# A two-stack transformer kernel: the FFN's down product runs two groups behind gate and up, and its first groups go through HBM

## Chip, cores and metric

One core of a Trainium2 chip runs one program. The metric is device microseconds (us) from start to end of an execution, median of three; lower is better. All arithmetic is float32; matmul operands are split into a high and a low part of a shorter type, and each product is three matmuls.

## Reference

Two stacks of two layers each work on one sequence of 256 tokens of width 1024. A layer is an FFN, a mixing part (attention and a gated recurrence, not touched here) and a second FFN, so there are eight FFNs. Cut to what matters:

```python
def swiglu(h, w_gate, w_up, w_down):            # w_gate, w_up: 1024 x 2816; w_down: 2816 x 1024
    return (jax.nn.silu(h @ w_gate) * (h @ w_up)) @ w_down

def hybrid_layer(x, ...):
    x = x + 0.5 * swiglu(rmsnorm(x, ffn1_norm), ffn1_wg, ffn1_wu, ffn1_wd)
    x = x + mixing(rmsnorm(x, mix_norm))        # projections, attention, recurrence, w_out
    x = x + 0.5 * swiglu(rmsnorm(x, ffn2_norm), ffn2_wg, ffn2_wu, ffn2_wd)
    return x
```

## The kernel before

All weights come from HBM in one stream of **units** of 1 MB (128 x 2048 floats), in the order of use. A unit passes four engines. SP (`load`, L317) starts its DMA into one of five `raw` buffers, once DVE has finished with the unit that held the buffer (`lo_done`). ACT (`split`, L815) copies it to one of three `w_hi` slots, once PE has used the unit three earlier (`used`). DVE (`split`, L1215) writes the remainder into `w_lo`. PE waits for `lo_done` and runs the unit's 24 matmuls of 512 columns.

An FFN has 11 groups of 256 hidden columns (`GROUPS`). Group g has three units: `front` and `back`, the two halves of gate and up over the 1024 inputs, and `down`, its 256 rows of the down matrix. `ffn_use` numbers them in the stream. Each engine's program is written out by hand and runs in that order; semaphores tie the engines together. The first FFN's units are called unit 0, 1, 2 and so on in this text.

Between gate/up and down, a group's 256 x 256 activations have to be computed and turned. ACT (`gates`, L877) takes the sigmoid from the two PSUM banks into `gate_s`, DVE (`gated`, L1260) multiplies twice and leaves `act` (semaphore `a_ready`). Then there are two ways to turn it:

- groups in `TURNED`: PE transposes `act` with four 128 x 128 matmuls into the bank `PT` (`turn_act`, L528). Before the change these are groups 0 and 10 of every FFN and group 1 of the first, 17 in all.
- groups in `EXCHANGED`: SP sends `act` to HBM (`spill`) and, after that has landed, reads it back in another order (`exchange`, L338); DVE finishes with 32 x 32 transposes (`act_turn`, L1271) into `act_t`. `act_t` and `gate_s` are the same SBUF bytes, so `gates` of the next group waits until `act_low` has read `act_t`.

Either way ACT writes `act_hi` (`act_high`, L888) and DVE `act_lo` (`act_low`, L1277; semaphore `alo_ready`), on which `down` waits. SP's exchange stands in the same queue as its weight loads: while it waits for `a_ready` or for the spill to land, no load is issued.

PSUM has eight banks: `PB` (0, 1) for gate/up, `PD` (2 to 5) for the down sums (and for gate/up of group 0), `PX` (6, 7), of which bank 6 is `PT`. Before the change every group from 1 on used `PB`.

In the first FFN, three small pieces of unrelated work are put between the groups: `tables(0)` to `tables(2)` on DVE after groups 1, 4 and 7 (`DVE_TABLES_AT`) and `tables(0)`, `tables(1)` on ACT after groups 2 and 5 (`ACT_TABLES_AT`). DVE's `tables(0)` is the run of operations from L1730 to L1753, ACT's holds three table loads. At the same time POOL loads constants and 16 pieces of `rpb` through its own DMA queue, and then adds masks to them.

Of the kernel before, what the change touches and what calls it, by code (L numbers as in the profile page):

```python
# [27 lines left out]
GROUPS = FF // 256  # L28
LAYERS = 2
UNIT = 2048  # L30
SLOTS, RAW = 3, 5
# [26 lines left out]
EXCHANGED = [at for at in ALL_GROUPS if 0 < at[3] < GROUPS - 1 and at != (0, 0, 0, 1)]  # L58
# [28 lines left out]
def build(nc, stream, xt, params, final_gain, code_w, gate_w, forget_w, rpb,  # L87
          lower, positions, forget_bias, c_square, c_level, c_col, c_att, c_freq, c_sel, c_reset, spill, out):
    ctx = ExitStack()
    with ctx:  # L90
# [90 lines left out]
        XB, PT = bank[0:2] + bank[6:8], bank[6]  # L181
# [80 lines left out]
        def ffn_no(b, L, j, g):  # L262
            return (4 * b + 2 * L + j) * GROUPS + g

# [146 lines left out]
        def _(pe):  # L411
# [81 lines left out]
            def ffn(b, L, j):  # L493
# [3 lines left out]
                def front(banks, g):  # L497
# [3 lines left out]
                    if g >= 2:  # L501
                        pe.wait_ge(a_ready, 2 * ffn_no(b, L, j, g))
# [309 lines left out]
        def _(act):  # L812
# [58 lines left out]
            def ffn(b, L, j):  # L871
# [5 lines left out]
                def gates(g):  # L877
                    if g >= 1:
                        act.wait_ge(alo_ready, ffn_no(b, L, j, g))
                    for t in range(2):  # L880
                        if t == 0:
                            act.wait_ge(tile_ready, ffn_no(b, L, j, g) + 1)
                        else:
                            act.wait_ge(used, use_of("back", g) + 1)
                        src = (PD if g == 0 else PB)[t][:, 0:256]
                        fn(gate_s[:, t, :], src, ACT.Sigmoid, scale=rms[:, t:t + 1]).then_inc(sig_done, 1)  # L886

                def act_high(g):  # L888
# [3 lines left out]
                    else:  # L892
                        act.wait_ge(act_turned, spill_no(b, L, j, g) + 1)
                        src = act_t
                    fn(act_hi[g % 2][:, :, :].rearrange("p a b -> p (a b)"), src, ACT.Copy).then_inc(ahi_ready, 1)  # L895
# [29 lines left out]
                for g in range(1, GROUPS):  # L925
                    act_high(g - 1)
                    split(use_of("front", g) + SLOTS)
                    gates(g)
                    split(use_of("back", g) + SLOTS)
                    if g == GROUPS - 1:  # L930
                        act_high(g)
                        table(EXP_LN_SET)
# [8 lines left out]
                    split(use_of("down", g - 1) + SLOTS)  # L941
# [266 lines left out]
        def _(dve):  # L1208
# [44 lines left out]
            def ffn(b, L, j):  # L1253
# [6 lines left out]
                def gated(g):  # L1260
                    no = ffn_no(b, L, j, g)
                    banks = PD if g == 0 else PB
# [54 lines left out]
                for g in range(1, GROUPS):  # L1317
                    if (b, L, j, g - 1) in EXCHANGED:
                        act_turn(g - 1)
                    act_low(g - 1)  # L1320
                    split(use_of("front", g) + SLOTS)
                    gated(g)
                    if g == GROUPS - 1:
                        split(use_of("back", g) + SLOTS)
                        act_low(g)
                    else:
                        split(use_of("back", g) + SLOTS)
# [6 lines left out]
                    if g < GROUPS - 1:  # L1334
                        split(use_of("down", g - 1) + SLOTS)
# [553 lines left out]
def weight_stream(i):  # L1889
# [5 lines left out]
    for b in range(2):  # L1895
        g1, u1, d1, w_in, w_out, g2, u2, d2 = (i[k] for k in names[b])
        for L in range(LAYERS):
            def ffn(j, g, u, d):
# [12 lines left out]
                gate_up(0)  # L1911
                for n in range(1, GROUPS):
                    gate_up(n)
                    down(n - 1)
# [65 lines left out]
```

## Time and profile before

| | us |
|---|---|
| median of 3 runs (lowest, highest) | 2010.35 (2009.53, 2012.16) |
| the profiled execution: its time, its span | 2007.96, 2006.2 |
| PE busy | 1983.8 (99% of the span) |
| DVE busy | 1374.9 (69%) |
| ACT busy | 1067.5 (53%) |

PE's matmuls overlap in the records: one lasts 0.39 us and the next starts 0.23 us after it, so that a PE that always shows busy may still lose small pieces of time between starts. Times inside the trace count from the span's start. The groups of rows below are quoted by number further on.

### The profile page before, as it was taken

The page shows a single profiled execution, that of the slowest core. Times are in us where ns is not written, and L with a number is a line of the kernel's source. Part 1 is how long each engine was busy: PE and PEld are TensorE (multiplying, and loading weights), DVE is VectorE, ACT ScalarE, POOL GpSimd, SP SyncE. Part 2 cuts the span into 40 slices and gives each one's busy share as a digit, 9 for nine tenths or more (in the row PEclk, how much of TensorE's full clock was granted, in tenths as well). Part 3 has the DMA queues.
Part 4 walks back from the last instruction along what each step waited for, and adds up shares of the span by engine and source line. Part 5 has one row for each costly group of instructions (what it writes and reads, how often), then busy time and mean ns, then how long its engine had stood idle before and what let it go on. Part 6 is the DMA issues. An engine that isn't in the chain of part 4 may idle for free.

```text
span 2006.2 us, 26785 instructions
## 1 busy us (share of the span) xinstructions
PE 1983.8 (99%) x10888; PEld 1663.8 (83%) x10888; DVE 1374.9 (69%) x1688; ACT 1067.5 (53%) x1357; POOL 55.6 (3%) x73
## 2 busy tenths in 40 slices
PE   8999999999999999999999999999999999999998
PEld 7888887888888887888888898888888889888887
DVE  6666976666666696766666669766666666976665
ACT  5545676444544567544554466654455445665444
POOL 3200004000000000000000000000000000000000
PEclk9999999999999999999999999999999999999999
DMA  9765437666566543666566644256656664425662
GB/s 321 249 222 188 162 113 211 228 221 228 193 232 225 177 150 105 220 225 229 195 217 230 227 156 169 107 203 221 227 193 221 227 230 159 168 106 210 221 221 83
DMA packets 145995, 395.62 MB, mean 197 GB/s; under 512 B 81808, under 2 KB 100496, under 8 KB 103504
## 3 DMA queue, kind: packets, MB, share of 16 engines
q1 hardware_dynamic: 142832, 387.49, 55.4%
q0 software_dynamic: 2608, 6.07, 1.4%
q8 instruction: 86, 1.41, 0.3%
q10 hardware_dynamic: 432, 0.35, 0.1%
q14 instruction: 37, 0.30, 0.0%
HBM read 374.21 MB, written 19.66 MB: 196 GB/s over the span
## 4 chain that ended last, share of the span: by engine, by line
PE 87%; DVE 7%; ACT 3%; DVEq 1%; DMA 1%; issue 1%; ACTq 0%; SPq 0%
PE bank L421 83%; DVE w_lo L1219 2%; PE bank L466 1%; PE bank L589 1%; ACT w_hi L821 1%; PE bank L673 1%; DVE arena L1347 1%; PE bank L657 1%; PE bank L635 1%; DMA spill<-scratch 0%; DVE arena L1434 0%; PE bank L603 0%; PE bank L532 0%; DMA x<-xt 0%; DVEq L1435 0%
## 5 line engine op out<-in xcount | busy, mean ns | idle before, releaser
L1219 DVE TENSOR_TENSOR w_lo<-raw,w_hi 128x2048 fp32r<-128x2048 f32 x330 | 757.6, 2297 | 379.5 <-ACT w_hi L821 378.9
L821 ACT ACTIVATE w_hi<-raw 128x2048 fp32r<-128x2048 f32 x330 | 629.7, 1910 | 246.1 <-PE bank L421 242.9
L421 PE MATMUL bank<-w_hi,h_hi 128*128 128x512 f32 x1536 | 602.5, 392 | 1.3 <-DVE arena L1511 0.8
L421 PE MATMUL bank<-w_hi,h_lo 128*128 128x512 f32 x1536 | 598.3, 390 | 0.0
L421 PE MATMUL bank<-w_lo,h_hi 128*128 128x512 f32 x1536 | 598.1, 389 | 0.0
L421 PEld LDWEIGHTS bank<-w_hi,h_hi 128*128 128x128 f32 x1536 | 288.6, 188 | 64.5 <-issue 2.7
L421 PEld LDWEIGHTS bank<-w_hi,h_lo 128*128 128x128 f32 x1536 | 288.5, 188 | 60.5
L421 PEld LDWEIGHTS bank<-w_lo,h_hi 128*128 128x128 f32 x1536 | 288.7, 188 | 58.8
L421 PE MATMUL bank<-w_hi,act_hi 128*128 128x512 f32 x832 | 327.8, 394 | 2.9 <-DVE act_lo L1568 2.1
L421 PE MATMUL bank<-w_hi,act_lo 128*128 128x512 f32 x832 | 324.2, 390 | 0.0
L421 PE MATMUL bank<-w_lo,act_hi 128*128 128x512 f32 x832 | 324.0, 389 | 0.0
L886 ACT ACTIVATE scratch<-bank,rms 128x256 f32<-128x256 f32 x176 | 83.2, 474 | 206.1 <-PE bank L421 206.0
L421 PEld LDWEIGHTS bank<-w_hi,act_hi 128*128 128x128 f32 x832 | 156.2, 188 | 36.9 <-DVE act_lo L1568 2.9
L421 PEld LDWEIGHTS bank<-w_hi,act_lo 128*128 128x128 f32 x832 | 156.2, 188 | 32.8
L421 PEld LDWEIGHTS bank<-w_lo,act_hi 128*128 128x128 f32 x832 | 156.3, 188 | 31.3
L895 ACT ACTIVATE act_hi<-scratch 128x512 fp32r<-128x512 f32 x71 | 45.0, 633 | 245.2 <-DVEq L1275 245.2
L421 PE MATMUL bank<-h_hi,w_hi 128*128 128x256 f32 x576 | 165.2, 287 | 0.0
L421 PE MATMUL bank<-h_lo,w_hi 128*128 128x256 f32 x576 | 162.8, 283 | 0.0
L421 PE MATMUL bank<-h_hi,w_lo 128*128 128x256 f32 x576 | 162.7, 283 | 0.0
L421 PEld LDWEIGHTS bank<-h_hi,w_hi 128*128 128x128 f32 x576 | 110.1, 191 | 3.9 <-issue 3.4
L421 PEld LDWEIGHTS bank<-h_hi,w_lo 128*128 128x128 f32 x576 | 110.2, 191 | 0.0
L421 PEld LDWEIGHTS bank<-h_lo,w_hi 128*128 128x128 f32 x576 | 110.2, 191 | 0.0
(213 smaller groups left out, 1403.4 us busy)
## 6 DMA issues: line engine op xcount, KB each, us to landing
raw<-stream SPq DMA_DIRECT2D x331, 1024.0 KB, 4.9
spill<-scratch SPq DMA_DIRECT2D x71, 256.0 KB, 3.7
scratch<-spill SPq DMA_DIRECT2D x71, 256.0 KB, 2.6
arena<-rpb POOLq DMA_DIRECT2D x32, 96.0 KB, 9.5
x<-xt SPq DMA_DIRECT2D x4, 256.0 KB, 5.5
raw<-stream SPq DMA_DIRECT2D x2, 512.0 KB, 5.9
arena<-final_gain POOLq DMA_DIRECT2D x2, 512.0 KB, 4.4
out<-x SPq DMA_DIRECT2D x3, 256.0 KB, 2.5
```

Source lines behind the costliest of these rows:

```text
L421: last = mm(o, a, r, start=start and n == 0, stop=stop and n == len(pairs) - 1)
L466: last = nc.tensor.transpose(XB[k // 2][:, (k % 2) * T + t * P:(k % 2) * T + (t + 1) * P], source[:, t, k * P:(k + 1) * P], ident)
L589: last = mm(PD[o][half, at:at + 64], src[rows, 1, ch, 64 * n:64 * n + 64], src[rows, 0, ch, 64 * m:64 * m + 64], start=True, stop=True)
L635: last = mm(PX[e][:, 0:n], aq[rows, hp, q], ak[rows, hp, 0:n], start=True, stop=True)
L657: last = nc.tensor.transpose(turn_bank(b, i)[:, n * P:(n + 1) * P], scratch[:, i % 2, n * P:(n + 1) * P], ident)
L673: last = mm(head_bank(b, i)[64 * e:64 * e + 64, 0:P], av[:, kt, hp * P + 64 * e:hp * P + 64 * e + 64], pT[:, i % 2, (2 * e + kt) * P:(2 * ...
L821: fn(w_hi[u % SLOTS][:, :], raw[u % RAW][:, :], ACT.Copy).then_inc(hi_done, 1)
L886: fn(gate_s[:, t, :], src, ACT.Sigmoid, scale=rms[:, t:t + 1]).then_inc(sig_done, 1)
L895: fn(act_hi[g % 2][:, :, :].rearrange("p a b -> p (a b)"), src, ACT.Copy).then_inc(ahi_ready, 1)
L1219: tt(w_lo[u % SLOTS][:, :], raw[u % RAW][:, :], w_hi[u % SLOTS][:, :].bitcast(F32), ALU.subtract).then_inc(lo_done, 1)
L1347: return tt(dst, a, r, ALU.subtract)
```

## The change

`ffn_use` and `weight_stream` put the down unit of group g behind gate and up of group g + 2 instead of g + 1. The order in the first FFN, by units, was front 0, back 0, front 1, back 1, down 0, front 2, back 2, down 1, ...; it becomes front 0, back 0, front 1, back 1, front 2, back 2, down 0, front 3, back 3, down 1, ..., back 10, down 8, down 9, down 10. Gate and up use `PD` for group 0, `PB` for odd groups and `PX` for even ones from 2 on. `EXCHANGED` takes in every group but the last, so 8 groups are left in `TURNED`. On ACT and DVE, groups 1 and 2 have both weight splits ahead of the turning of the group before; later groups have one ahead of it.

```diff
-EXCHANGED = [at for at in ALL_GROUPS if 0 < at[3] < GROUPS - 1 and at != (0, 0, 0, 1)]
+EXCHANGED = [at for at in ALL_GROUPS if at[3] < GROUPS - 1]
...
-        XB, PT = bank[0:2] + bank[6:8], bank[6]
+        XB, PT = bank[0:2] + bank[6:8], bank[0]
...
             if kind == "down":
-                off = 3 * g + 4 if g < GROUPS - 1 else FFN_UNITS - 1
+                off = 3 * g + 6 if g < GROUPS - 2 else FFN_UNITS - GROUPS + g
             else:
-                off = (3 * g - 1 if g else 0) + (kind == "back")
+                off = (3 * g - 2 if g else 0) + (g == 1) + (kind == "back")
...
+        def gate_banks(g):
+
+            return PD if g == 0 else PB if g % 2 else PX
...
-                    if g >= 2:
-                        pe.wait_ge(a_ready, 2 * ffn_no(b, L, j, g))
+                    if g >= 3:
+                        pe.wait_ge(a_ready, 2 * ffn_no(b, L, j, g - 1))
...
-                front(PD, 0)
-                back(PD, 0)
-                for g in range(1, GROUPS):
-                    front(PB, g)
-                    if (b, L, j, g - 1) in TURNED:
-                        turn_act(g - 1)
-                    back(PB, g)
-                    down(g - 1, {(0, 3): lambda: turn_act(GROUPS - 1)} if g == GROUPS - 1 else {})
+                for g in range(GROUPS):
+                    front(gate_banks(g), g)
+                    back(gate_banks(g), g)
+                    if g >= 2:
+                        down(g - 2)
+                turn_act(GROUPS - 1)
+                down(GROUPS - 2)
...
                 for g in range(1, GROUPS):
+                    split(use_of("front", g) + SLOTS)
+                    if g < 3:
+                        split(use_of("back", g) + SLOTS)
                     if (b, L, j, g - 1) in EXCHANGED:
                         act_turn(g - 1)
                     act_low(g - 1)
-                    split(use_of("front", g) + SLOTS)
                     gated(g)
+                    if g >= 3:
+                        split(use_of("back", g) + SLOTS)
```

DVE in the first FFN before the change, from the gating of group 0 on. L1265/L1269 are `gated`, L1280 is `act_low`, L1219 a weight split; `raw0` here holds unit 5, `raw1` unit 6, `raw2` unit 7:

```order
L1219 TENSOR_TENSOR w_lo2<-raw0,w_hi2 128x2048 [waits hi_done]
L1265 SCALAR_TENSOR_TENSOR scratch<-bank,rms,scratch 128x256 [waits sig_done]
L1269 SCALAR_TENSOR_TENSOR scratch<-bank,rms,scratch 128x256 [waits at_ready]
L1265 SCALAR_TENSOR_TENSOR scratch<-bank,rms,scratch 128x256 [waits sig_done]
L1269 SCALAR_TENSOR_TENSOR scratch<-bank,rms,scratch 128x256
L1219 TENSOR_TENSOR w_lo0<-raw1,w_hi0 128x2048 [waits hi_done]
L1730 CAST arena<-cos_sin 128x256 [waits table_loaded]
...
L1753 TENSOR_SCALAR cos_sin<-arena 128x256 x2
L1219 TENSOR_TENSOR w_lo1<-raw2,w_hi1 128x2048 [waits hi_done]
```

and of the changed kernel (L1286 is `act_turn`, L1231 a weight split, L1744 to L1767 are `tables(0)`):

```order
L1231 TENSOR_TENSOR w_lo2<-raw0,w_hi2 128x2048 [waits hi_done]
L1231 TENSOR_TENSOR w_lo0<-raw1,w_hi0 128x2048 [waits hi_done]
L1286 STREAM_TRANSPOSE scratch<-scratch 128x4x2x32 [waits act_back]
L1286 STREAM_TRANSPOSE scratch<-scratch 128x4x2x32
L1292 TENSOR_TENSOR act_lo0<-scratch,act_hi0 128x512 [waits ahi_ready]
L1277 SCALAR_TENSOR_TENSOR scratch<-bank,rms,scratch 128x256 [waits sig_done]
...
L1744 CAST arena<-cos_sin 128x256 [waits table_loaded]
...
L1767 TENSOR_SCALAR cos_sin<-arena 128x256 x2
L1231 TENSOR_TENSOR w_lo1<-raw2,w_hi1 128x2048 [waits hi_done]
```

The turning of group 0 now waits for a DMA (`act_back`), and `tables(0)` and the split of unit 7 come behind it.

ACT at the same place before the change (L895 is `act_high`, L886 `gates`, L821 a weight split, `raw4` holds unit 9, `raw0` unit 10):

```order
L895 ACTIVATE act_hi1<-bank 128x512 [waits at_ready]
L821 ACTIVATE w_hi2<-raw3 128x2048 [waits used,raw_ready3]
L886 ACTIVATE scratch<-bank,rms 128x256 [waits tile_ready,alo_ready]
L886 ACTIVATE scratch<-bank,rms 128x256 [waits used]
L821 ACTIVATE w_hi0<-raw4 128x2048 [waits used,raw_ready4]
L833 ACT_TABLE_LOAD
...
L821 ACTIVATE w_hi1<-raw0 128x2048 [waits used,raw_ready0]
```

and of the changed kernel (L900 `act_high`, L889 `gates`, L824 a weight split):

```order
L900 ACTIVATE act_hi1<-scratch 128x512 [waits act_turned]
L889 ACTIVATE scratch<-bank,rms 128x256 [waits tile_ready,alo_ready]
L889 ACTIVATE scratch<-bank,rms 128x256 [waits used]
L836 ACT_TABLE_LOAD
L1179 ACTIVATE cos_sin<-cos_sin 128x512 [waits ang_ready]
L836 ACT_TABLE_LOAD
L1181 ACTIVATE lbt<-lbt 128x8
L836 ACT_TABLE_LOAD
L824 ACTIVATE w_hi0<-raw4 128x2048 [waits used,raw_ready4]
```

The split of unit 9 stood ahead of ACT's tables and now stands behind them.

## Rows read from the trace of the kernel before

**Rows 1.** Chain that ended last, one piece of the second FFN: start, us, what, matmuls.
```profile
339.18 155.09 PE bank L421 x684
```

**Rows 2.** Timeline of PE around two turned groups: start, us, engine, line, what [idle before].
```profile
338.35 0.39 PE L421 MATMUL bank<-w_hi,h_lo 128*128 128x512 f32 x1
...
339.73 0.39 PE L421 MATMUL bank<-w_hi,h_hi 128*128 128x512 f32 x1
...
1012.39 0.60 PE L532 MATMUL bank<-square,scratch 128*128 128x128 f32 x4
1013.18 0.50 PE L421 MATMUL bank<-w_hi,h_hi 128*128 128x512 f32 x1 [0.19 <-DVE w_lo L1219]
```

**Rows 3.** The line of the PE transposes, its instructions over the whole span.
```profile
L532 PE MATMUL bank<-square,scratch x68: 270/272/273, 28.0 to 1990.8; 128*128 128x128 f32 x68
```

**Rows 4.** Timeline of PE in the first FFN: unit 2's last matmul, unit 11's first.
```profile
27.81 0.39 PE L421 MATMUL bank<-w_hi,h_lo 128*128 128x512 f32 x1
...
73.32 0.47 PE L421 MATMUL bank<-w_hi,h_hi 128*128 128x512 f32 x1 [0.27 <-DVE scratch L1269]
```

**Rows 5.** Timeline of DVE in the first FFN.
```profile
27.04 0.48 DVE L1269 SCALAR_TENSOR_TENSOR scratch<-bank,rms,scratch 128x256 f32<-128x256 f32 x1
...
38.69 0.44 DVE L1730 CAST arena<-cos_sin 128x256 f32<-128x256 int32 x1
...
44.90 2.27 DVE L1219 TENSOR_TENSOR w_lo<-raw,w_hi 128x2048 fp32r<-128x2048 f32 x1
...
59.98 2.94 DVE L1219 TENSOR_TENSOR w_lo<-raw,w_hi 128x2048 fp32r<-128x2048 f32 x1 [4.41 <-ACT w_hi L821]
64.74 1.10 DVE L1274 STREAM_TRANSPOSE scratch<-scratch 128x256 f32<-128x256 f32 x2 [1.82 <-DMA scratch<-spill]
66.57 0.69 DVE L1280 TENSOR_TENSOR act_lo<-scratch,act_hi 128x512 fp32r<-128x512 f32 x1 [0.73 <-ACT act_hi L895]
...
71.19 0.47 DVE L1265 SCALAR_TENSOR_TENSOR scratch<-bank,rms,scratch 128x256 f32<-128x256 f32 x1
...
73.09 4.49 DVE L1219 TENSOR_TENSOR w_lo<-raw,w_hi 128x2048 fp32r<-128x2048 f32 x2
```

**Rows 6.** Timeline of ACT in the first FFN.
```profile
39.66 1.92 ACT L821 ACTIVATE w_hi<-raw 128x2048 fp32r<-128x2048 f32 x1 [3.22 <-PE bank L421]
...
53.27 1.28 ACT L833 ACT_TABLE_LOAD   x1
...
58.03 1.92 ACT L821 ACTIVATE w_hi<-raw 128x2048 fp32r<-128x2048 f32 x1
...
68.25 0.81 ACT L886 ACTIVATE scratch<-bank,rms 128x256 f32<-128x256 f32 x2
```

**Rows 7.** DMA issues, last figure us to landing: unit 8's load; an exchange at 393:402.
```profile
25.64 0.33 SPq L321 DMA_DIRECT2D raw<-stream  x1
raw<-stream SPq DMA_DIRECT2D x1, 1024.0 KB, 9.3
...
spill<-scratch SPq DMA_DIRECT2D x1, 256.0 KB, 3.6
scratch<-spill SPq DMA_DIRECT2D x1, 256.0 KB, 2.6
```

**Rows 8.** DMA queues at 38:40 (q0 is POOL's, q1 SP's): packets, MB, share.
```profile
q0 software_dynamic: 145, 0.36, 93.3%
q1 hardware_dynamic: 18, 0.08, 14.1%
```

**Rows 9.** PE's timeline, early and last; a window: length, busy by engine, clock, DMA.
```profile
11.36 0.63 PE L421 MATMUL bank<-w_lo,h_hi 128*128 128x512 f32 x1
11.79 0.63 PE L421 MATMUL bank<-w_hi,h_lo 128*128 128x512 f32 x1
...
1998.87 0.39 PE L421 MATMUL bank<-w_hi,act_lo 128*128 128x512 f32 x1
...
2002.50:2003.00 0.50, 0.00 (x0) 0.00 (x0) 0.00 (x0) 0.16 (x1) 0.00 (x0) 0.50 0.00 0
```

More of the change, by code:

```diff
@@ L884, in gates @@
                             act.wait_ge(used, use_of("back", g) + 1)
[L885 removed]
+                        src = gate_banks(g)[t][:, 0:256]
                         fn(gate_s[:, t, :], src, ACT.Sigmoid, scale=rms[:, t:t + 1]).then_inc(sig_done, 1)
@@ L894, in act_high @@
                         src = act_t
+                    if g >= 2:
+                        act.wait_ge(used, use_of("down", g - 2) + 1)
                     fn(act_hi[g % 2][:, :, :].rearrange("p a b -> p (a b)"), src, ACT.Copy).then_inc(ahi_ready, 1)
@@ L925, in ffn @@
                 for g in range(1, GROUPS):
+                    split(use_of("front", g) + SLOTS)
+                    if g < 3:
+                        split(use_of("back", g) + SLOTS)
                     act_high(g - 1)
-                    split(use_of("front", g) + SLOTS)
                     gates(g)
-                    split(use_of("back", g) + SLOTS)
+                    if g >= 3:
+                        split(use_of("back", g) + SLOTS)
                     if g == GROUPS - 1:
                         act_high(g)
+                        split(use_of("down", g - 2) + SLOTS)
                         table(EXP_LN_SET)
@@ L940, in ffn @@
                         fn(code_hi[:, :], w, ACT.Copy).then_inc(code_split, 1)
-                    split(use_of("down", g - 1) + SLOTS)
+                    if 2 <= g < GROUPS - 1:
+                        split(use_of("down", g - 2) + SLOTS)
+                    if g == GROUPS - 1:
+                        split(use_of("down", g - 1) + SLOTS)
             def evict_pair(b, L, i, t):
@@ L1261, in gated @@
                     no = ffn_no(b, L, j, g)
-                    banks = PD if g == 0 else PB
+                    banks = gate_banks(g)
                     for t in range(2):
@@ L1317, in ffn @@
                 for g in range(1, GROUPS):
+                    split(use_of("front", g) + SLOTS)
+                    if g < 3:
+                        split(use_of("back", g) + SLOTS)
                     if (b, L, j, g - 1) in EXCHANGED:
@@ L1320, in ffn @@
                     act_low(g - 1)
-                    split(use_of("front", g) + SLOTS)
                     gated(g)
+                    if g >= 3:
+                        split(use_of("back", g) + SLOTS)
                     if g == GROUPS - 1:
-                        split(use_of("back", g) + SLOTS)
                         act_low(g)
-                    else:
-                        split(use_of("back", g) + SLOTS)
+                        split(use_of("down", g - 2) + SLOTS)
                     if (b, L, j, g) in DVE_TABLES_AT:
@@ L1333, in ffn @@
                         tt(code_lo[:, :], w, code_hi[:, :].bitcast(F32), ALU.subtract).then_inc(code_split, 1)
-                    if g < GROUPS - 1:
-                        split(use_of("down", g - 1) + SLOTS)
+                    if 2 <= g < GROUPS - 1:
+                        split(use_of("down", g - 2) + SLOTS)
             def halves(ap, m):
@@ L1909, in down @@
                         out.append(rows.reshape(4, 2, 32, D).transpose(0, 2, 1, 3).reshape(P, UNIT))
-                gate_up(0)
-                for n in range(1, GROUPS):
+                for n in range(GROUPS):
                     gate_up(n)
-                    down(n - 1)
+                    if n >= 2:
+                        down(n - 2)
+                down(GROUPS - 2)
                 down(GROUPS - 1)
```

## The prediction, made blind

> **What bounds the kernel now.** I read the page's busy shares first: PE 99% of the span, everything else under 70%. Then the chain that ended last: nearly all of it is PE, in long unbroken pieces. Inside an FFN 684 matmuls take 155.09 us, 0.2267 us each [rows 1], so a unit of 24 takes 5.44 us, and nothing that only gives the other engines more slack can shorten that. The list of waits shows PE idle behind other engines only twice inside the FFNs, for 0.27 and 0.19 us [rows 2, 4]. So the change can win only the PE instructions that it removes, and can lose wherever one of the other engines becomes late. I therefore read the timelines of DVE, ACT and SP where slack is smallest: the first FFN, where `tables`, POOL's loads and the first exchanges meet.
>
> **Part 1: nine groups less transposed on PE.** 68 transposes are 17 groups [rows 3]; 8 are left. From the start of the last matmul ahead of one to that of the fourth behind it, 338.35 to 339.73 are 1.38 us where four steps of 0.2267 make 0.91 [rows 2]: a group costs 0.47 us. Two of the nine lie in the first FFN and are in part 2. Of the other seven, the one at 1012.39 gives nothing: PE stands behind it for the split of the next unit, and that unit starts at 1013.18 either way, since neither ACT nor DVE gets to that split sooner [rows 2]. Six are left: 6 x 0.47 = 2.8 us gained.
>
> **Part 2: the first FFN.** I step through it to unit 11, which is front 4 in both orders and started at 73.32 [rows 4]. Undisturbed, the units after 27.81 + 0.23 = 28.04 come every 5.44 us [rows 1, 4]: unit 4 at 38.9, unit 6 (now down 0) at 44.4, unit 7 (front 3) at 49.8, unit 9 (down 1) at 60.7, unit 11 at 71.6.
>
> Call X0 the time at which DVE starts turning group 0. It cannot be sooner than the two splits put ahead of it: the second is unit 6's, whose slot is free when PE ends unit 3, at 28.04 + 5.44 = 33.5. ACT starts 0.26 us behind a unit's end and takes 1.92 (as at 39.66) [rows 6], and DVE's step of 2.2 follows (two in 4.49) [rows 5]: X0 is at least 37.9. It also needs the readback. The gating of group 0 ends at 27.04 + 0.48 = 27.5 [rows 5], and the spill is issued then, behind unit 8's load, which was issued at 25.64 and landed 9.3 us later, at 34.9 [rows 7]. I let the spill land 1.1 us after that, 36.0. The readback takes 2.6 us when free [rows 7]; POOL's `rpb` pieces begin then, so I take 3.3: X0 = 39.3. The bounds are 37.9 and 42. The upper one is by the queue rows, where SP's queue had 14.1% of the DMA engines against POOL's 93.3% from 38 to 40, just when the readback is to land [rows 8].
>
> The Trainium skill ("DMA: Bandwidth & Descriptors", Queues, rings and completion order) says that a DMA engine takes turns between its queues packet by packet. By that rule the small readback would not be starved and X0 would be near 39.3, total 2015.0 us; by the queue rows taken literally X0 is 42, total 2017.5.
>
> From X0 the chain is serial. `act_low` ends 2.5 us after the start of the turning (64.74 to 66.57 + 0.69) [rows 5]; down 0 needs it at 44.4 and has it at 41.8. The sigmoids follow, and the four gating operations take 1.9 (71.19 to 73.09) [rows 5], half a microsecond after the first sigmoid: gating ends at X0 + 5.0. Then `tables(0)`, 38.69 to 44.90, 6.2 us [rows 5], and only then unit 7's split, 2.3 us. Unit 7 can start at X0 + 5.0 + 6.2 + 2.3 + 0.1 = X0 + 13.6 = 52.9, not 49.8: **first stall, 3.1 us**. Before, unit 7's split had nothing but a finished transpose ahead of it.
>
> The next turning, X1, waits for the splits of units 7 and 8, X0 + 11.2 + 4.4 = 54.9, and for exchange 1, whose spill is issued at 44.3 behind the loads of units 9 and 10, held back until SP had seen the first spill land. I take X1 = 55.3. From there `act_low` 2.6, two sigmoids 0.8 [rows 6], ACT's tables 4.8 (53.27 to 58.03) [rows 6], unit 9's high split 1.9, its low split 2.3, or 2.9 where POOL works as at 59.98 [rows 5], 0.1 to start: 12.5 to 13.2, I take 12.9. Unit 9 starts at 68.2. With unit 7 at 52.9 it would have started at 63.8: **second stall, 4.4 us**. Unit 11 then starts at 68.2 + 10.9 = 79.1. A third stall does not come: the split of unit 11 ends 7.5 us after the turning of group 2, which follows unit 10's split at about 71, so at 78.5.
>
> **Part 3: the clock.** Early on, matmuls start 0.43 us apart (11.36, 11.79) instead of 0.23 [rows 9]: the lower of TensorE's two levels, 1.2 GHz, after PE had hardly worked. At the end the last matmul is over at 1999.3, and from 2002.5 on the granted clock is 0.50 [rows 9], about 3.2 us later. The second stall is longer than that, the first about as long. If some eight matmuls then run 0.2 us slower each, that is 1.6 us; the other bound is nothing. I take 1.6: unit 11 at 80.7, against 73.32 that is 7.4 us lost. The Trainium skill ("TensorE: Matmul & The Clock Gate", Part 1) says that an idle TensorE falls back to 1.2 GHz and that work releases it again; by it the sum is 2015.0 us, and without a fall it is 2013.4. The trace's end agrees with its first half.
>
> **Part 4: the other seven FFNs.** There are no tables there and POOL's loads are few. In group 3 the slack is smallest: the turning of group 2 needs the readback, some 6.2 us (3.6 + 2.6) after its gating ends [rows 7]. Counting as above from the end of unit 2, turning of group 0 at +9.9, of group 1 at +21.3 (9.9 + 5.0 + 6.2 and a little), of group 2 at +32.6; unit 11's split is done 7.5 later, at +40.1, and it is wanted at +43.5. The slack of 3.4 covers even an exchange 2 us slower in either place. From group 4 on the low split of the back unit is done 4 us ahead. The last groups have the transposes behind down 8, where `act` has been ready for over a microsecond. Nine more exchanges add 4.6 MB of DMA, hidden. Each of these costs nothing; what it costs where the cover is gone is the next to last rival.
>
> **Sum.** -2.8 + 7.4 = +4.6 us. The profiled execution's 2007.96 becomes 2012.6; it lay 2.4 us under the median of the runs shown, so the median should go from 2010.35 to 2015.0.
>
> **Rivals.**
> - *Not slower: the first exchange comes back early.* If the spill is not held up by unit 8's load, X0 is 37.9, X1 53.5, unit 9 starts at 66.1 and unit 11 at 77.0; with no fall of the clock that is +3.7 - 2.8 = +0.9, 2011.3 us. For it: 3.6 and 2.6 us are all that an exchange needs when free [rows 7]. Against it: one queue, and 1 MB ahead. It decides as long as X0 is under 40.3 without a fall of the clock, under 38.7 with one.
> - *DMA slower than I take it.* X0 = 42, X1 = 57.6, unit 9 at 70.8, unit 11 at 81.7 + 1.6: +10.0 - 2.8 = +7.2, 2017.5 us. The queue rows speak for it [rows 8].
> - *The later FFNs stall too.* Some 1 us at group 3 in each of seven: 2022 us. Against it: the slack of 3.4.
> - *The start hides it all.* Nine groups at 0.47 us and a smoother start: -4.2 - 0.9, 2005.3 us. It needs unit 7's split done by 49.7, hence X0 under 36.2, which the two splits ahead of it forbid as far as I can see, and DVE's tables out of the way.
>
> **How the numbers follow.** The forecast has 0.40, the early exchange 0.33, slower DMA 0.14, later stalls 0.06, the faster case 0.07. About 0.2% (4.0 us) is what a measurement of this kernel can tell from no change, so the bound lies at 2014.4, next to my forecast: its own range is 2012.8 to 2016.8, and a quarter of it falls within. Slower is 0.30 + 0.14 + 0.06 = 0.50, within 0.2% is 0.33 + 0.10 = 0.43, faster 0.07. The range takes in the early exchange and the slow one, each a little widened for the scatter of the median: 2010.6 to 2018.5.
>
> **What the changed profile would show.** Parts 1 and 4: 32 transposes on the line of `turn_act`, and each later FFN shorter by 0.47 us but the fifth. Part 2: DVE's turning of group 0 starts near 39.3; PE idle for about 3 us ahead of unit 7 (near 50) and over 4 us ahead of unit 9 (near 64), released by the low split; ACT's tables right ahead of that split. Part 3: a granted clock under 1 behind the second gap. I am wrong in the large if PE waits in the later FFNs, or if the gaps near 50 and 64 are missing.

## The result, and the profile after

| | before | after |
|---|---|---|
| median (lowest, highest), us | 2010.29 (2009.53, 2012.16) | 2019.61 (2019.05, 2022.57) |
| the profiled execution: its time, its span | 2007.96, 2006.2 | 2019.18, 2017.4 |

The changed kernel is slower, by a ratio of 1.0054 (95% interval 1.0042 to 1.0066), 9.3 us in the medians and 11.2 us between the two profiled executions. The prediction was 2015.0 with a range up to 2018.5: the sign was right, the size too small. POOL is the engine that the expectations below call GpSimd.

In PE's list of waits (us in total, times, longest) the row of PE behind the weight splits was the last of the kernel before, with one wait of 0.2 us. In the changed kernel it stands first:

```profile
PE bank L425 <- DVE w_lo L1231: 10.6, 3, 5.8
```

PE's timeline shows the three waits, ahead of unit 7, ahead of unit 9, and a small one in the fifth FFN (start, us, engine, line, what, [idle before]):

```profile
50.60 0.39 PE L425 MATMUL bank<-w_hi,act_lo 128*128 128x512 f32 x1
55.20 0.80 PE L425 MATMUL bank<-w_hi,h_hi 128*128 128x512 f32 x1 [4.21 <-DVE w_lo L1231]
...
67.52 0.39 PE L425 MATMUL bank<-w_hi,h_lo 128*128 128x512 f32 x1
73.68 0.77 PE L425 MATMUL bank<-w_hi,act_hi 128*128 128x512 f32 x1 [5.78 <-DVE w_lo L1231]
...
87.15 0.39 PE L425 MATMUL bank<-w_hi,h_hi 128*128 128x512 f32 x1
...
1025.47 0.50 PE L425 MATMUL bank<-w_hi,h_hi 128*128 128x512 f32 x1 [0.60 <-DVE w_lo L1231]
```

The row at 87.15 is unit 11, counted 48 matmuls on from 73.68: 13.8 us later than at 73.32 before [rows 4]. What stood ahead of it is best read in the chain of the changed kernel between 40 and 80 us (start, us, what):

```profile
35.51 6.57 DMA scratch<-spill
42.10 0.63 DVE scratch L1286
...
47.17 10.38 DMA spill<-scratch
57.57 2.70 DMA scratch<-spill
60.30 0.65 DVE scratch L1286
...
62.12 1.54 DVE act_lo L1292
...
64.55 1.28 ACT L836
...
69.30 1.92 ACT w_hi L824
71.25 2.30 DVE w_lo L1231
```

Two exchanges, 6.6 us for a readback and 10.4 us for a spill, are what PE waited for at the second gap; then ACT's tables and the split of unit 9. The queues of the changed kernel at 36 to 38 us, right behind the issue of that readback, answer to [rows 8]; SP's queue q1 does not appear at all. Part of that silence is the transfer's own start: in the version below that only keeps POOL's loads away ("only POOL's loads clean"), the readback was issued at 34.76 and q1's packets begin after 36.0. In the changed kernel it was issued at 35.51, and they begin after 38.0. The second row is q1 in that version, at the same 36 to 38:

```profile
q0 software_dynamic: 104, 0.21, 106.8%
...
q1 hardware_dynamic: 298, 0.48, 77.2%
```

To see how much of the 11.2 us lies in the first FFN, I use a mark in PE's timeline, the transposes of `x` for the next norm, which stand near the end of every FFN and of every mixing part. Before and after, the marks that end the first FFN, the first mixing part and the second FFN:

```profile
192.23 1.03 PE L466 MATMUL bank<-square,x 128*128 128x128 f32 x8
...
318.93 1.03 PE L466 MATMUL bank<-square,x 128*128 128x128 f32 x8
...
501.40 1.03 PE L466 MATMUL bank<-square,x 128*128 128x128 f32 x8
```

```profile
205.97 1.03 PE L470 MATMUL bank<-square,x 128*128 128x128 f32 x8
...
332.67 1.03 PE L470 MATMUL bank<-square,x 128*128 128x128 f32 x8
...
514.66 1.03 PE L470 MATMUL bank<-square,x 128*128 128x128 f32 x8
```

From 318.93 to 501.40, the second FFN took 182.47 us; now 181.99. The first product of the kernel started at 10.79 before and at 11.41 after, so the first FFN took 181.44 us up to its mark and now takes 194.56. The account of the span: first product 0.62 later, first FFN 13.12 longer, and all the rest 2.54 shorter, 11.2 in sum. From mark to mark, six of the seven later FFNs are about 0.5 us shorter, the fifth is not (182.91 and 182.90), and the last mixing part is 0.4 longer. The change does what it was to do in the other FFNs and loses it five times over in the first.

This account belongs to the two profiled executions. That of the kernel before was 2.3 us faster than its median, that of the changed kernel 0.4; no trace shows where a median execution of the kernel before spends its 2.3 us.

### The profile page after: what moved, and what is told of

Same layout as the page of the kernel before. It is cut to its first block, busy times and chain, and to the rows that moved or that the text cites. A ratio compares the mean times of both kernels' runs of the same rounds, so it can differ in the third digit from the quotient of the medians.

```text
span 2017.4 us, 26822 instructions
## 1 busy us (share of the span) xinstructions
PE 1984.4 (98%) x10852; PEld 1663.0 (82%) x10852; DVE 1384.2 (69%) x1706; ACT 1066.3 (53%) x1357; POOL 52.3 (3%) x73
## 4 chain that ended last, share of the span: by engine, by line
PE 85%; DVE 7%; ACT 3%; DMA 2%; DVEq 1%; issue 1%; ACTq 0%; SPq 0%
PE bank L425 81%; DVE w_lo L1231 2%; ACT w_hi L824 1%; PE bank L470 1%; DMA spill<-scratch 1%; PE bank L592 1%; PE bank L676 1%; DVE arena L1361 1%; PE bank L660 1%; DMA raw<-stream 1%; PE bank L638 1%; DMA scratch<-spill 0%; DVE arena L1448 0%; PE bank L606 0%; DVEq L1449 0%
## 5 line engine op out<-in xcount | busy, mean ns | idle before, releaser
L1231 DVE TENSOR_TENSOR w_lo<-raw,w_hi 128x2048 fp32r<-128x2048 f32 x330 | 756.5, 2294 | 352.5 <-ACT w_hi L824 352.1
L824 ACT ACTIVATE w_hi<-raw 128x2048 fp32r<-128x2048 f32 x330 | 631.0, 1914 | 379.7 <-PE bank L425 376.5
L900 ACT ACTIVATE act_hi<-scratch 128x512 fp32r<-128x512 f32 x80 | 50.6, 632 | 284.4 <-DVEq L1287 284.4
L1277 DVE SCALAR_TENSOR_TENSOR scratch<-bank,rms,scratch 128x256 f32<-128x256 f32 x176 | 84.4, 480 | 46.5 <-ACT scratch L889 46.5
```

What stands on the lines that cost most here:

```text
L824: fn(w_hi[u % SLOTS][:, :], raw[u % RAW][:, :], ACT.Copy).then_inc(hi_done, 1)
L1231: tt(w_lo[u % SLOTS][:, :], raw[u % RAW][:, :], w_hi[u % SLOTS][:, :].bitcast(F32), ALU.subtract).then_inc(lo_done, 1)
L1277: stt(gate_s[:, t, :], banks[t][:, 0:256], rms[:, t:t + 1], gate_s[:, t, :], ALU.mult, ALU.mult)
```

## The experiments

"First FFN" below is this length, from the first product to the first mark. The first matmuls run at the lower clock for a time that differs from run to run: unit 0's 24 took between 6.1 and 7.3 us in these traces, and unit 1 always 5.44. So lengths of the first FFN compare to some 1.2 us only; counted from unit 1 they compare much better, and I give both where it matters. The length of the second FFN repeats to 0.02. A gap "start to start" is 0.39 longer than the idle time in the same row's brackets. Ratios are against the kernel before, measured with each group of versions; its medians there were 2009.27, 2009.22, 2010.02 and 2009.22, and the ratio need not be the quotient of the medians to the last digit.

### GpSimd's bias loads later

Two theories had to be told apart. Either the exchanges are starved by POOL's queue (DMA), or the work put ahead of the splits on DVE and ACT (the tables) is too long however fast the exchanges are. First POOL's sixteen `rpb` loads were held back until the sixteenth split unit; in this version's trace they were issued from 97.39 on:

```diff
+                if L == 0:
+                    pool.wait_ge(lo_done, 16)
```

> The changed kernel with one edit: POOL starts its 16 rpb pieces only when DVE has split unit 15, so they no longer share the DMA engines with the first two exchanges. Theory A (the DMA: the gaps ahead of units 7 and 9 come from the exchanges of groups 0 and 1 waiting behind POOL's pieces): the readback of group 0 takes 3 us instead of 6.6 and the spill of group 1 about 4 instead of 10.4, and both gaps go, 2005 us. Theory B (the order on DVE and ACT: the tables stand between the turned group and the split that PE needs): nothing changes, 2019 us. What I expect is that both hold, one behind the other: the turning of group 0 starts near 39, unit 7 is 2 us late and unit 9 another 4 us, 2012 us.

Measured: 2011.09 us, ratio 1.0004 (0.9995 to 1.0013); first FFN 188.31. The stalls went from 4.2 and 5.8 us idle to 1.0 and 3.4. The sixth exchange, issued at 107.1, now met the loads and its spill took 10.2 us, but PE did not wait for it.

### The tables later

The tables moved to later groups, POOL where it was:

```diff
-DVE_TABLES_AT = {(0, 0, 0, 1): 0, (0, 0, 0, 4): 1, (0, 0, 0, 7): 2}
-ACT_TABLES_AT = {(0, 0, 0, 2): 0, (0, 0, 0, 5): 1}
+DVE_TABLES_AT = {(0, 0, 0, 4): 0, (0, 0, 0, 6): 1, (0, 0, 0, 9): 2}
+ACT_TABLES_AT = {(0, 0, 0, 5): 0, (0, 0, 0, 7): 1}
```

> The changed kernel with the tables of the first FFN moved back: on DVE from behind groups 1, 4, 7 to 4, 6, 9, on ACT from behind groups 2 and 5 to 5 and 7. POOL's loads stay. Theory B (order): both gaps go, 2005 us. Theory A (DMA): the two gaps stay as they are, 2019 us. Both together: no gap ahead of unit 7, since its split follows the gating of group 1 at once; ahead of unit 9 the exchange of group 1, which takes 13 us, still leaves a gap of about 6.5 us, and the clock falls behind it; 2014 us.

Measured: 2016.04 us, ratio 1.003 (1.0019 to 1.0041); first FFN 192.15. As expected, no gap is left ahead of unit 7. But the first readback took 9.0 us this time, so that PE waited 1.6 us ahead of down 0, which I had not foreseen, and the gap ahead of unit 9 was 8.1 us idle where I expected 6.5. With no table anywhere near, DVE's timeline still shows 9.9 us of waiting for exchange 1, whose spill was issued at 49.28 and its readback only at 61.04 (DVE's timeline, then PE's):

```profile
63.82 1.09 DVE L1286 STREAM_TRANSPOSE scratch<-scratch 128x256 f32<-128x256 f32 x2 [9.90 <-DMA scratch<-spill]
```

```profile
46.77 0.50 PE L425 MATMUL bank<-w_hi,act_hi 128*128 128x512 f32 x1 [1.62 <-DVE act_lo L1292]
...
71.52 0.77 PE L425 MATMUL bank<-w_hi,act_hi 128*128 128x512 f32 x1 [8.12 <-DVE w_lo L1231]
```

### Both

> The changed kernel with both edits, POOL's rpb pieces behind unit 15 and the tables moved back. If the two causes together are all of the loss, PE has no gap in the first FFN and the clock stays at its full level: unit 11 starts near 72.4 against 84.6, nothing runs at half speed, 14.9 us less than the changed kernel, 2004.7 us, and 5 us less than the kernel before. If something else of the change costs time in the first FFN (banks, more exchanges in SP's queue), it stays above 2008 us.

Measured: 2007.13 us, ratio 0.9989 (0.998 to 0.9998). (The 84.6 in the expectation is not unit 11's start in the changed kernel, which is at 87.15.) No gap up to 120 us, but there one that I had not foreseen. PE's and SP's timelines of this kernel:

```profile
120.44 0.39 PE L427 MATMUL bank<-w_hi,h_lo 128*128 128x512 f32 x1
122.93 0.50 PE L427 MATMUL bank<-w_hi,h_hi 128*128 128x512 f32 x1 [2.10 <-DVE w_lo L1233]
```

```profile
98.39 0.38 SPq L346 DMA_DIRECT2D spill<-scratch  x1
111.69 0.38 SPq L348 DMA_DIRECT2D scratch<-spill  x1
```

POOL issued its loads from 91.50 to 101.8, and the spill at 98.39 took 13.3 us until its readback could go out, where all others behind the first took 2.6 to 5.4. The starved exchange had only moved with the loads.

### Groups 0 and 1 of the first FFN transposed by PE again

```diff
+                    if g >= 2 and (b, L, j, g - 2) in TURNED:
+                        pe.wait_ge(alo_ready, ffn_no(b, L, j, g - 2) + 1)
```

(with `EXCHANGED` without these two groups, and a transposed group's bank taken from its own pair, which needs this wait ahead of the front that reuses the bank)

> The changed kernel, but groups 0 and 1 of the first FFN alone are turned by PE's transposes again (bank 6 for group 0, bank 0 for group 1), as in the kernel before; down stays two groups behind, tables and POOL as they are. If only the exchanges of these two groups start the loss, the gap ahead of unit 7 goes, that ahead of unit 9 shrinks to about 1 us by the tables on ACT, and the six later FFNs keep their 0.5 us each: 2007 us. If moving down or the two splits is what costs (theory C), it stays near 2015 to 2019 us.

Measured: 2012.3 us, ratio 1.0012 (1.0003 to 1.0021), missed by 5 us, and by my own edit. One gap, at 34 us:

```profile
39.67 0.52 PE L429 MATMUL bank<-w_hi,h_hi 128*128 128x512 f32 x1 [4.99 <-DVE act_lo L1300]
```

`act_lo` of group 0 stands behind the second of the two splits, that of unit 6, whose slot PE gives back only at the end of unit 3; front 2 of PE now waited for it. Transposing the first groups and two splits ahead don't go together. So the same with one split ahead (`split(use_of("back", g) + SLOTS)` behind `gates`/`gated` for every g), together with two controls and the version that the gap at 120 us suggested: POOL's loads behind the last exchange of the first FFN.

### A clean start, and the kernel before with the same

```diff
                 if L == 0:
-                    pool.wait_ge(lo_done, 16)
+                    pool.wait_ge(act_back, 16 * 10)
```

(tables as in the version with both)

> The changed kernel with the rotary and decay tables behind later groups (DVE behind 4, 6 and 9, ACT behind 5 and 7) and with GpSimd's sixteen loads of the position bias held until the tenth and last exchange of the first FFN has landed (about 170 us), where no exchange follows before attention. Theory A (all that the change loses is exchanges of the first FFN that GpSimd's queue starves, plus tables ahead of an exchange's turning): no start gap over 0.8 us between 30 and 190 us, every exchange 2.6 us each way, the 2.5 us gap at 120 us of the version with both moved is gone; span 2001.5, time 2004.7 (2003.5 to 2005.7). Rival B (two groups behind is itself short of slack in the first FFN): the gap at 120 us stays, time 2007. Rival C (the late loads meet attention instead): a new wait for the bias or for the codes at 205 to 230 us, time 2006 to 2009.

Measured: **2004.56 us, ratio 0.9975 (0.9965 to 0.9985)**, faster than both kernels. First FFN 179.33, second 181.99; the chain of this kernel has 31 of the first FFN's 33 units in one piece, 744 matmuls at 0.2274 us:

```profile
12.11 169.15 PE bank L427 x744
```

> Control: the kernel before, with the same two moves (tables behind later groups; GpSimd's bias loads behind the last exchange of its first FFN). Theory A: its first FFN had only one start gap of 0.66 us and hardly a fall of the clock, so these moves bring it nothing: 2009.3, ratio 0.999 to 1.001; against it the changed kernel with a clean start is 4.5 us faster, which is then the worth of the change itself. Rival: the moves help both alike, 2006 to 2007, and the change alone is worth 2 us or less.

Measured: 2009.47 us, ratio 1.0002 (0.9993 to 1.001). First FFN 181.34, against 181.44 without the two moves. That looks like nothing gained, but unit 0 was slower in this trace (7.16 against 6.37); counted from unit 1 the first FFN took 174.18 against 175.07, so the two moves bring the kernel before 0.9 us there, against my expectation. The changed kernel with a clean start has 173.20, another 0.98 less, which is two groups at 0.49. The control lost something that I had not put in the expectation: its last exchange is later, POOL added its masks until 216.0, and DVE was slower beside it. Four scans at 213.82 took 3.89 us, at 211.98 in the version with a clean start, where the masks were done at 198.6, 2.44. PE then waited 2.15 us for DVE (DVE's timeline, then PE's). The mixing part behind the first FFN took 128.90 instead of 126.70, the only other place where this trace differs from the kernel before. Without that the control would be near 2007.3, by my estimate from these rows. So the 4.9 us between the two medians are not all the worth of the change: some 2.2 are the control's late masks, and 2.7 are left; the traces' pieces (0.98 in the first FFN and 2.5 behind it) give 3.5. A control with the masks out of the way was not run.

```profile
213.82 3.89 DVE L1436 TENSOR_TENSOR_SCAN arena<-reset,arena 128x256 f32<-128x256 f32 x4
```

```profile
219.67 0.52 PE L591 MATMUL bank<-arena 64*64 64x64 f32 x20 [2.15 <-DVEq L1395]
```

> Control: the kernel before, with GpSimd's bias loads held until the sixteenth split weight unit (about 91 us), tables where they were. Theory A: the loads then meet the exchange that starts at about 98 us, which takes some 13 us instead of 3.6; with the down product one group behind there is less slack than two behind (2.1 us of idle there in the changed kernel), so PE idles 3 to 8 us once and the clock falls after it: 2012 to 2019. Rival: exchanges of the kernel before are not starved, 2009.5.

Measured: 2014.6 us, ratio 1.0024 (1.0014 to 1.0033). The old kernel is starved in the same way once the loads meet one of its exchanges: a spill of 14.2 us, where its others in the first FFN take 3.4 to 4.8. PE idled 5.49 us, where two groups behind had 2.10 with the tables moved (a spill of 13.3 us) and nothing with the tables in place (10.2 us). That fits less slack with the down product one group behind; but the spills differ in length and the loads began at different times (88.5, 91.5 and 97.4), so the slack by itself is not shown.

```profile
101.51 0.38 SPq L342 DMA_DIRECT2D spill<-scratch  x1
115.71 0.38 SPq L344 DMA_DIRECT2D scratch<-spill  x1
```

```profile
121.70 0.80 PE L423 MATMUL bank<-w_hi,act_hi 128*128 128x512 f32 x1 [5.49 <-DVE act_lo L1282]
```

> The changed kernel with groups 0 and 1 of the first FFN transposed by PE and only one weight split ahead of the first groups' act_hi and act_lo (which took the wait for unit 4 in the version with groups 0 and 1 transposed). Theory A: neither the exchanges of groups 0 and 1 nor the splits are in the way, so no start gap over 1 us between 30 and 60 us, clock 1.00 in 40:90, 2006 to 2007.5. Rival (down two groups behind loses in the first FFN by itself): a gap of 3 us or more ahead of unit 7 or 9 stays, 2010 or more.

Measured: 2007.93 us, ratio 0.9994 (0.9985 to 1.0003). Loads and tables stand where the changed kernel has them, yet there is no gap between 12 and 190 us: without the exchanges of groups 0 and 1 nothing in the start is late. Down two groups behind loses nothing in the first FFN. But PE now waited 3.0 us for weight splits in three places of later FFNs. One of these, 0.60 us in the fifth FFN, the changed kernel has as well; the other two, 1.80 and 0.62 us ahead of the down product of group 0 in the second and fifth FFN, came with one split ahead.

### One split ahead; and only POOL's loads clean

```diff
                     split(use_of("front", g) + SLOTS)
-                    if g < 3:
-                        split(use_of("back", g) + SLOTS)
...
-                    if g >= 3:
-                        split(use_of("back", g) + SLOTS)
+                    split(use_of("back", g) + SLOTS)
```

> The version with the clean start, with only one weight split ahead of the first groups' turning, act_hi and act_lo (in every FFN): the second split is put back behind them. Theory A (the first exchange of an FFN stands behind raw loads on SP's queue for some 9 us, and the second split is work that fills DVE and ACT in that time): a gap of about 2 us ahead of the down product of group 0 in some of the later FFNs, as the version with one split and two transposed groups showed three times (2.2, 1.0 and 1.0 us); 2007.5 (2006.5 to 2008.5), so the two splits are worth 2 to 3.5 us. Rival (the gaps there came from the first groups' transposes): 2004.6.

Measured: 2007.03 us, ratio 0.9988 (0.9979 to 0.9997); second FFN 183.67, against 181.99 with two splits. The wait ahead of its down 0, and SP's timeline before it:

```profile
357.22 0.47 PE L427 MATMUL bank<-w_hi,act_hi 128*128 128x512 f32 x1 [1.44 <-DVE w_lo L1230]
```

```profile
325.86 10.19 SPq L325 DMA_DIRECT2D raw<-stream  x3
337.63 0.38 SPq L346 DMA_DIRECT2D spill<-scratch  x1
345.94 0.38 SPq L348 DMA_DIRECT2D scratch<-spill  x1
```

The first exchange of an FFN stands behind unit loads on SP's own queue. But the 8.3 us here are not theirs alone: POOL loads the other sixteen of its 32 `rpb` pieces in the second FFN and adds masks to them there, in every version. POOL's timeline, and DVE's `act_lo` of group 0 beside the masks:

```profile
312.15 10.37 POOL L399 DMA_DIRECT2D arena<-rpb  x16
...
343.34 8.19 POOL L403 TENSOR_TENSOR arena<-arena,col_mask 128x384 f32<-128x384 f32 x8 [20.82 <-DMA arena<-rpb]
```

```profile
350.47 1.61 DVE L1291 TENSOR_TENSOR act_lo<-scratch,act_hi 128x512 fp32r<-128x512 f32 x1 [0.73 <-ACT act_hi L902]
```

The three unit loads ahead of the spill took 11.8, 10.0 and 9.4 us to land, where 4.9 is this kernel's median, and `act_lo` took 1.61 instead of 0.69. In the six FFNs without such loads the first spill took 4.0 to 5.9 us. There, one split ahead cost PE no wait in this version: PE's three waits for a split, 2.7 us in sum, are 0.69 ahead of down 0 of the first FFN, the 1.44 above, and 0.61 in the fifth FFN, which the version with two splits has too (0.62). With two splits, the spill of the second FFN took 8.8 us; DVE's second split ended as the readback had landed, near 347.5, and PE did not wait. So what the second split covers is the time of that exchange.

> The changed kernel with GpSimd's bias loads behind the last exchange of the first FFN, and the tables where they were. Theory A: the tables of 5.8 us on DVE and the table load on ACT still stand ahead of the turning of group 1 and of the splits: gaps of about 1.4 us ahead of unit 7 and 3.8 us ahead of unit 9, the clock lower after the second, as in the version with those loads at 91 us; 2011.0 (2009.8 to 2012.2). With the version that moves tables alone (2016.0) and the one that moves both (2004.6) this makes the square of the two causes. Rival (tables matter only beside a starved exchange): 2006 or less.

Measured: 2011.81 us, ratio 1.0007 (0.9998 to 1.0016). The gaps are those foreseen, 1.40 and 3.78 from start to start (1.02 and 3.39 idle), and the clock follows the second: twelve starts are 0.43 us apart, and unit 9 takes 2.9 us more than at full clock. PE's timeline, and then windows of this kernel (stretch, length, busy PE, PEld, DVE, ACT, POOL, clock, DMA share, GB/s):

```profile
51.79 0.50 PE L427 MATMUL bank<-w_hi,h_hi 128*128 128x512 f32 x1 [1.02 <-DVE w_lo L1233]
...
66.40 0.76 PE L427 MATMUL bank<-w_hi,act_hi 128*128 128x512 f32 x1 [3.39 <-DVE w_lo L1233]
```

```profile
64.00:66.00 2.00, 0.00 (x0) 0.00 (x0) 2.00 (x1) 1.72 (x1) 0.00 (x0) 0.86 1.02 426
66.00:68.00 2.00, 1.60 (x4) 1.34 (x5) 2.00 (x2) 0.00 (x0) 0.00 (x0) 0.50 0.30 74
```

With this the square is full. Length of the first FFN (181.44 before the change):

| | tables early | tables late |
|---|---|---|
| POOL's loads among the exchanges | 194.56 (the change) | 192.15 |
| POOL's loads behind them | 188.08 | 179.33 |

The loads cost 12.8 us with the tables out of the way and 6.5 with them in it; the tables cost 8.8 and 2.4. Counted from unit 1, the four lengths are 187.78, 185.25, 180.99 and 173.20 (175.07 before the change), the loads cost 12.1 and 6.8 and the tables 7.8 and 2.5: the same picture. They lie partly beside each other, so the two causes of 15.2 us (14.6 from unit 1) can't be split into shares, and either alone keeps more than half of the loss. DVE's and ACT's tables were always moved together, so their parts were not told apart.

### Only the depth

Last, the clean start with group 0 of every FFN transposed by PE and one split ahead.

> The clean start and one split ahead, with the first group of every FFN transposed by PE in a bank of its own group's pair instead of exchanged; only the down product two groups behind, and the exchange of group 1 of the first FFN, are left of the change. Theory A (a step of four transposes costs PE 0.47 us, the down product two groups behind costs and gives nothing): eight such steps are 3.8 us over the best version's 2004.6, and no gap ahead of the down product of group 0: 2008.4 (2007.4 to 2009.4), so that the first exchanges with two splits are worth some 3.5 to 4 us, and without the two splits (2007.0) only 1.4. Rival (it is the depth that gains, the transposes are hidden): 2005.

Measured: 2007.08 us, ratio 0.9989 (0.998 to 0.9998), 0.3 us below my range. The step itself came out as expected: from mark to mark the second FFN takes 182.48 us, as before the change (182.47), against 181.99 with the exchange.

```profile
317.85 0.60 PE L476 MATMUL bank<-square,x 128*128 128x128 f32 x4
...
500.33 0.71 PE L476 MATMUL bank<-square,x 128*128 128x128 f32 x5
```

Counted from the first product, its span is 1994.4 against 1990.6 of the version with a clean start, 3.8 us longer. That this is eight times 0.47 is chance. From mark to mark, seven FFNs (the first counted from unit 1) are 0.49 longer, 3.4 in sum, and the fifth is not (182.90 in both), where without the transposes PE waits for a split instead; the last mixing part is 0.4 shorter, and unit 0 took 0.7 longer. My eight steps should have been seven. The depth itself costs and gives nothing here: the rival, at 2005, is out.

## Why the prediction was right and wrong

**What bounds the kernel, and Part 1, the transposes: right.** 32 transposes are left, and a later FFN is 0.48 us shorter (182.47 to 181.99), where the forecast said 0.47 and only six of seven FFNs: 2.54 us measured for 2.8. The rest of the 2.8 is in the last mixing part, 0.4 us longer, where PE waits 0.41 us once for ACT. The FFN that I said would give nothing gave nothing: the fifth took 182.91 us from mark to mark before and 182.90 after, because PE now waits 0.60 us there for the split for which it waited 0.19 behind the transposes.

**Part 4, the later FFNs: right in the result, wrong in one premise.** No new wait appeared there but the 0.60 us of the fifth FFN. I wrote that POOL's loads are few in the later FFNs; half of its `rpb` pieces, sixteen of 32, run in the second. There the first spill took 7.6 us in the changed kernel, where the other later FFNs have 4.0 to 6.0. That this cost nothing is due to the second split ahead of the turning: with one split, PE waited 1.44 us in the second FFN. My sum of 6.2 us for an exchange (3.6 + 2.6) was of a free one.

**Part 2, the first FFN: right places, sizes too small.** This is the step that failed: the time of the first two exchanges beside POOL's loads. I put the readback of exchange 0 near its free time, 3.3 us, and it took 6.6; exchange 1 then started 2.9 us later and took 2.1 us longer than I had it. By its own terms:

- *X0, forecast 39.3 (37.9 to 42), was 42.10.* The spill behind unit 8's load was about right: issued at 28.34, it landed at 35.5, 0.5 us before I had it, and took 7.2 us in the version without POOL's loads too. The readback is what I mis-sized: 6.6 us, not 3.3. Where the loads were gone it took 3.3, and DVE started the turning at 38.71, as soon as the second split let it.
- *First stall, forecast 3.1, was 4.2 idle.* It follows from X0 and made no difference in the end, since the second stall is set by X1. X0 itself did: the spill of exchange 1 is issued 5.1 us behind it.
- *X1, forecast 55.3, was 60.30.* I let the splits and the exchange tie at 55. The splits were done at 57.35, but exchange 1 set the time. Its spill was issued at 47.17 instead of 44.3, 2.9 us later because of X0; and from issue to X1 it took 13.1 us where I had 11.0, 10.4 of them for the spill. The spill stood behind two unit loads issued at 35.93 and 36.45, which POOL's queue had held up (11.8 and 17.7 us to land), and landed 3.4 us after the second of these. Without POOL's loads the same spill took 2.6 us. I had counted POOL against the first exchange only, and not against the loads ahead of the second. X1 is the largest term, 5.0 of the 6.45 us by which unit 11 missed its forecast of 80.7, and more than half of it comes from the readback of exchange 0.
- *From X1 to unit 9: 13.4, forecast 12.9* (`act_lo` took 1.53 instead of 0.69 while POOL added its masks).
- *What the trace of before already held.* In it one spill stands behind unit loads just as POOL's loads end, and it took 9.4 us; in the control with these loads later, the spill issued at the same 52.5 took 4.6. I took my figures for an exchange from a quiet stretch (3.6 and 2.6 us) and never used this row (chain: start, us, what):

```profile
52.55 9.39 DMA spill<-scratch
```

- *Unit 4.* The list of undisturbed starts has it at 38.9, which is its end; it starts at 33.5. No time hangs on it.
- *The name of unit 11.* I called it front 4 in both orders. In the changed order it is back 4; the stepping went by unit numbers, so no time hangs on it.

**Part 3, the clock: right mechanism, too small.** Forecast 1.6 us, measured 2.6: from 73.68 to 78.94 twelve matmuls start, 0.57 us apart once and then 0.43. The windows of the changed kernel around the second stall:

```profile
70.00:72.00 2.00, 0.00 (x0) 0.00 (x0) 0.76 (x1) 2.00 (x2) 0.00 (x0) 1.00 1.01 337
72.00:74.00 2.00, 0.32 (x1) 0.35 (x2) 2.00 (x2) 1.01 (x1) 0.00 (x0) 0.52 0.75 311
...
78.00:80.00 2.00, 2.00 (x8) 1.53 (x7) 1.38 (x4) 1.79 (x3) 0.00 (x0) 0.77 1.00 401
```

PE's last matmul ended at 67.9 and the granted clock was at its lower level, 1.2 GHz, from about 72; it was back at 79. The rule of the Trainium skill ("TensorE: Matmul & The Clock Gate", Part 1), that an idle engine falls back and work releases it, agrees with these rows. The first stall did the same from 55 to 58, and that cost was swallowed by the second.

**The number came nearer than the sum.** For the step itself I forecast +4.6 us; it was 11.2 between the profiled executions and 9.3 in the medians. To 2012.6 I added the 2.4 us by which the profiled execution lay under its median, as if every kernel had that distance; in the changed kernel it was 0.4. These 2.0 us hid part of the error of Part 2, and that was luck.

**The rivals.** "DMA slower than I take it" had X0 right at 42 and was still 2 us short of the median, because its X1, 57.6, again let only the splits decide. It had 0.14. The queue rows of before [rows 8] showed q1 at 14% beside q0 at 93%, which was in my hands, and I took the value near the free exchange, with the rule of the Trainium skill ("DMA: Bandwidth & Descriptors", Queues, rings and completion order) standing beside it. That rule, turns packet by packet, would have had X0 near 39.3; the measurement is 42.10, and it decides. The two need not contradict each other, though this is argued and not shown: at 36 to 38 us 104 packets of POOL's filled 106.8% of 16 engines, 0.33 us for each at a mean of 2 KB, while q1's packets at 34 to 36 (165 packets, 0.04 MB) are of about 0.25 KB. Equal turns of so unequal length leave the small packets little.

"The start hides it all", at 2005.3 with a chance of 0.07, is close to the time that the kernel has with a clean start, 2004.56; but that kernel has tables and loads in other places, so the rival did not come true. What I held against it, that the splits forbid X0 under 36.2, is true; with the tables gone X0 near 38.7 is early enough.

**What stays open.** How POOL's loads starve the others (the packet sizes above) was not tried by itself, for example with `rpb` loads in longer runs. Which of the unit loads ahead of it hold up the first exchange of an FFN was not tried either, nor what the second FFN would take with POOL's second sixteen loads placed elsewhere. What the change is worth with a clean start stays between 2.7 us (medians, less the control's masks) and 3.5 (pieces of the traces).

## What to carry to other kernels

When work is moved onto a DMA, price it in the stretch where it will run, and price what stands ahead of it on its own queue under the same load: here the readback with no load ahead of it lost 3.3 us to POOL's loads, and the spill with two held-up 1 MB loads ahead of it lost 7.8. Look for the same transfer under the same load in the trace that you have: the kernel before held a spill of 9.4 us. Filler (tables, constant loads) that costs nothing beside one schedule has to be placed again when the schedule changes; moving it was worth 15 us here and turned +0.5% into -0.25%. Check all places where the filler runs: half of POOL's loads ran in the second FFN, which I had taken as free of them. A filler that is moved must be followed to its new place as well: at 91 us it met another exchange, and behind the last one it was late for attention in the old kernel.

## What the runs showed of the hardware that I had not expected

- Sixteen loads of 96 KB on POOL's queue stretched whatever SP's queue had under way: a readback from 3.3 to 6.6 us (9.0 in the version with the tables later), spills of 256 KB from 2.6 to 10.4, 11.8 and 13.3 us, and from some 3.6 to 14.2 in the kernel before.
- A spill of 256 KB issued shortly behind unit loads on the same queue took longer than the 2.6 us that most take: 7.2 us behind unit 8's load at the start, and 3.9 to 6.6 us as the first of a later FFN in which POOL loads nothing.
- After six idle stretches of PE in these traces the clock was at its lower level for the next matmuls. The unit behind took longer by 2.9 us (3.4 idle), 1.7 (4.2 idle), 2.1 (5.0 idle), 1.7 (5.5 idle), 2.6 (5.8 idle) and 1.8 (8.1 idle): the price did not grow with the stretch. After 2.1 us idle, in the version with both moved, it did not fall.
- DVE is slower while POOL adds its masks: `act_lo` of 128 x 512 took 1.53 us instead of 0.69, four scans of 128 x 256 took 3.89 instead of 2.44, which delayed PE by 2.15 us in the control. In the versions where the masks came at another time, both had their shorter times.
